# A two-layer block in split single precision: the rows of both operand buffers start at other addresses

## What is computed

```python
h = rms_norm(r, g_mix); z = h @ w_in                     # q, k, v, conv and gate columns
attn = moba_attention(q, k, v)                           # 8 heads of 128, one block of 256 keys
r = r + (sigmoid(g_a) * (attn @ w_attn_out) + sigmoid(g_c) * (conv @ w_conv_out)) @ w_o
r = r + square(relu(rms_norm(r, g_mlp) @ w_up)) @ w_down # width 8192
r = r + sigmoid(rms_norm(r, g_ple) @ w_ple_gate) * (p @ w_ple_proj)
# second layer, 16 more tokens ahead of the 256
u = conformer_conv(h)        # h @ conv_w_in, gate, 31 taps in time, layer norm, silu, @ conv_w_out
r = r + swiglu(h)            # (silu(h @ ffn_w_gate) * (h @ ffn_w_up)) @ ffn_w_down, width 5632
```

## Time and profile before

| | |
|---|---|
| three runs | 2543.49, 2543.50, 2542.21 us, median 2543.49 |
| profiled execution | span 2542.0 us from first to last instruction; 1.49 us less than the median of the runs. No other time is given for this execution |
| busy | PE 2523.6 us (99%), weight loads 2224.7 (88%), DVE 1722.5 (68%), ACT 1252.9 (49%), POOL 431.3 (17%) |
| read from HBM | 463 MB, 183 GB/s over the span |

### The profile page before, as it was taken

One profiled execution on the slowest core, in us unless ns is written; L12 is line 12 of the kernel. 1 busy time (PEld: TensorE's weight loads), 2 busy tenths in 40 slices (PEclk: granted clock), 3 DMA queues, 4 the chain that ended last, 5 costly groups with the idle time before them and its releaser, 6 DMA issues.

```text
span 2542.0 us, 42618 instructions
## 1 busy us (share of the span) xinstructions
PE 2523.6 (99%) x14605; PEld 2224.7 (88%) x14605; DVE 1722.5 (68%) x2097; ACT 1252.9 (49%) x1554; POOL 431.3 (17%) x291
## 2 busy tenths in 40 slices
PE   9999999999999999999999999999999999999998
PEld 8888888888888888888888899988888888888887
DVE  6568875587665665665667889985766556654665
ACT  6456555554544444444444554555644444444443
POOL 0034410002100000000002368973400000000001
PEclk9999999999999999999999999999999999999999
DMA  7655565665556666656565566536466656556554
GB/s 235 185 168 180 165 189 181 197 194 178 188 183 192 187 188 189 189 190 189 183 193 185 183 171 170 166 109 206 150 197 200 195 177 198 185 191 187 183 182 163
DMA packets 470962, 466.38 MB, mean 183 GB/s; under 512 B 14522, under 2 KB 441012, under 8 KB 470708
## 3 DMA queue, kind: packets, MB, share of 16 engines
q1 hardware_dynamic: 470336, 464.97, 59.1%
q10 hardware_dynamic: 546, 0.38, 0.1%
HBM read 463.20 MB, written 2.10 MB: 183 GB/s over the span
## 4 chain that ended last, share of the span: by engine, by line
PE 90%; DVE 8%; issue 1%; ACT 1%; POOL 0%; DMA 0%; DVEq 0%; POOLq 0%; ACTq 0%
PE gp L450 49%; PE gp L453 22%; DVE xp L1839 6%; PE gp L818 3%; PE gp L816 3%; PE gp L817 3%; PE gp L459 3%; PE gp L488 1%; PE gp L630 1%; PE gp L631 1%; PE gp L490 1%; PE gp L632 1%; PE xp L777 0%; DVE gp L1804 0%; DVE wlo L1423 0%
## 5 line engine op out<-in xcount | busy, mean ns | idle before, releaser
L1423 DVE TENSOR_TENSOR wlo<-stage,whi 128x1024 fp32r<-128x1024 f32 x809 | 1010.0, 1263 | 676.3 <-ACT whi L879 670.7
L879 ACT ACTIVATE whi<-stage 128x1024 fp32r<-128x1024 f32 x874 | 914.1, 1057 | 929.0 <-PE gp L453 601.7
L450 PE MATMUL gp<-A,whi 128*128 128x512 f32 x3968 | 1320.5, 393 | 0.3 <-DVE A L1530 0.3
L453 PE MATMUL gp<-A,wlo 128*128 128x256 f32 x3264 | 915.1, 280 | 0.0
L450 PEld LDWEIGHTS gp<-A,whi 128*128 128x128 f32 x3968 | 739.1, 188 | 164.1 <-DVE A L1530 0.7
L453 PEld LDWEIGHTS gp<-A,wlo 128*128 128x128 f32 x3264 | 614.5, 188 | 0.0
L450 PE MATMUL gp<-B,whi 128*128 128x512 f32 x1536 | 536.3, 394 | 0.6 <-issue 0.6
L453 PE MATMUL gp<-B,wlo 128*128 128x256 f32 x1536 | 430.5, 280 | 0.0
L450 PEld LDWEIGHTS gp<-B,whi 128*128 128x128 f32 x1536 | 287.7, 187 | 66.8 <-issue 1.0
L453 PEld LDWEIGHTS gp<-B,wlo 128*128 128x128 f32 x1536 | 290.2, 189 | 0.0
L2144 POOL TENSOR_TENSOR sq<-r 128x512 f32 x24 | 29.5, 1228 | 795.7 <-DVE r L1733 757.9
(11 more groups left out here) (324 smaller groups left out, 2143.5 us busy)
## 6 DMA issues: line engine op xcount, KB each, us to landing
stage<-in_w_in SPq DMA_DIRECT2D x160, 512.0 KB, 4.1
stage<-in_w_up SPq DMA_DIRECT2D x128, 512.0 KB, 3.8
stage<-in_w_down SPq DMA_DIRECT2D x128, 512.0 KB, 3.6
stage<-in_ffn_w_gate SPq DMA_DIRECT2D x88, 512.0 KB, 4.5
stage<-in_ffn_w_up SPq DMA_DIRECT2D x88, 512.0 KB, 4.4
stage<-in_ffn_w_down SPq DMA_DIRECT2D x88, 512.0 KB, 4.5
stage<-in_conv_w_in SPq DMA_DIRECT2D x64, 512.0 KB, 4.1
stage<-in_w_o SPq DMA_DIRECT2D x32, 512.0 KB, 4.4
```

The source lines that it names most:

```text
L450: nc.tensor.matmul(bank.rearrange("p (a t) -> p a t", a=2), hi, both_parts(M, kt), start=first, stop=False)
L453: done = nc.tensor.matmul(bank[:, T:2 * T], lo, M[:, kt, 0:T], start=False, stop=last)
L879: nc.scalar.activation(unit_homes(n, slot)[0], stage[:, slot, :], ACT.Copy).then_inc(hi_ready, 1)
L1423: nc.vector.tensor_tensor(lo, stage[:, slot, :], hi.bitcast(F32), ALU.subtract).then_inc(lo_ready, 1)
```

## The change

Each row of `A` becomes 548 words (2192 bytes in place of 2176) and each row of `B` 520 words (2080 in place of 2048). The low half stays at the same distance behind the high half. `both_parts` and `sq_parts` cut off the added words, so every instruction reads and writes as many elements as before, in the same order on each engine. Counted from the start of its buffer, row kt of `A` moves back by 16·kt bytes, row kt of `B` by 32·kt bytes. All that lies behind `A` moves by 256 bytes, and all behind `B` by 768 bytes in sum.

```diff
-        A = sb("A", [P, KT, 2 * TM], F32R)
-        B = sb("B", [P, KT, 2 * T], F32R)
+        A = sb("A", [P, KT, 2 * TM + 4], F32R)
+        B = sb("B", [P, KT, 2 * T + 8], F32R)
...
-        sq_parts = B[:, KT - 2:KT, :]
+        sq_parts = B[:, KT - 2:KT, 0:2 * T]
...
         def both_parts(M, kt):

-            return M[:, kt, :].rearrange("p (a t) -> p a t", a=2)[:, :, 0:T]
+            return M[:, kt, 0:2 * (TM if M is A else T)].rearrange("p (a t) -> p a t", a=2)[:, :, 0:T]
```

## The result

The changed kernel takes 2556.38 us (median of 4 runs, 2553.85 to 2556.78) against 2543.49 us before (4 runs, 2542.21 to 2543.67): a ratio of 1.005, 95% interval 1.0038 to 1.0062. It is slower by 12.9 us; the forecast was +1.9 us, the range held it. The profiled execution took 2556.09 us with a span of 2554.3 us, 12.3 us more than the span before.

What follows compares the result with a forecast made beforehand. The prediction took PE as the bound, the time being the sum of distances between matmuls. Its parts, −0.7 for B's pairs and +2.6 for back, the rest 0, gave +1.9 us on 2543.5: 2545.4 us, range 2518 to 2580.

Steps and rivals of the forecast that it cites:

- spread costs what A and v show: Whole kernel: spread rows of B take the distances that A's pairs and v's weights show; +1.9 us, chance 0.35.
- line of 5.1 us: Whole kernel: about 0.2%, what a measurement can tell from no change; slower than that was given 0.33.
- Pairs with B: 1536 pairs reading B: all take A's 348.4 ns, together −0.7 us, bounds −3.3 and +7.3.
- Pairs with A: 4096 pairs reading A: spread already, so 0, bounds −9.4 and +18.9 us.
- back: 1008 matmuls with rows of B stationary: 2.6 ns longer each, +2.6 us, bounds 0 and +2.6.
- v: 192 matmuls with rows of A stationary: 0, bounds −0.5 us and 0.
- conv2: Conv2's tiles, where the chain runs on DVE's taps: 0; with 3.4 ns on each matmul, +2 us.
- Other engines: DVE ops writing A and transfers into `stage`: hidden under PE, 0.
- Faster: All phases: differing starts break the slow rhythms and settle at the best distance seen; −13.2 us, 2530 us, chance 0.31.
- Slower: All pairs run like up's slow first round, 353.6 ns; +31 us, 2574 us, chance 0.28.
- harsher form: Pairs with A and B: starts between multiples of 64 bytes cost an extra piece, 6.7 ns; 2616 us.
- Addresses do nothing: Whole kernel: row places don't matter and differences are rhythm alone; 2543.5 us, chance 0.06.

Runs made afterwards that it cites:

- the moved starts alone: Kernel before with 64 unused words behind A and 128 behind B, rows unchanged: 2543.46 us, ratio 1.000.
- `B` alone moved: Kernel before with only B's rows eight words longer, A's rows unchanged: 2549.25 us, ratio 1.0025.
- `A` alone: Kernel before with only A's rows four words longer, B's rows unchanged: 2548.48 us, ratio 1.0017.
- the rows at multiples of 64 bytes: Kernel before with rows of A and B 16 words longer and a DMA scratch of 1024 bytes: 2555.23 us, ratio 1.0047.
- `A` at one place: Kernel before with A's rows of 2304 bytes, low half right behind the high half, B unchanged: 2543.34 us, ratio 1.0002.

## Why the prediction was right in kind and short in size

The reading of the bound held: no wait, transfer or other engine came into play but for PE's pause in conv2, and the time is the sum of distances that depend on where rows lie. The forecast "spread costs what A and v show" is the case that came, and the marks it set were met for up (349.5 to 349.9, "near 348 in all four rounds", a little high), down and glu (348 to 350), but not for back (232.7, "near 229"). The sum was +1.9 us in place of +12.3 in the profiles, and the time lies outside the forecast's own range (2540 to 2553) and inside the whole one. That the whole range held 2556.4 is luck as far as the forecast goes: its ends came from the rivals. By the prediction's own line of 5.1 us the kernel is slower, to which it gave 0.33, and 0.05 of that by the forecast's mechanism. By its steps:

1. *Pairs with B*: −0.7 forecast, +1.2 measured. Right that the quick pairs get slower and the slow ones quicker and nearly cancel. The size that was off is 348.4: it came out at 349.5. Both sums lean on the slow rhythm of up's first round in the profile before; against a quick one, as with the moved starts alone, that round would lose 0.75 us instead of gaining 0.95.
2. *Pairs with A*: 0 forecast, +3.4. The step that failed is "they are spread already". `A` had two places for its high halves, with its own mean, and got sixteen: down +1.4 ns a pair. Glu's later rounds lost nothing (−0.11 and −0.08 us), since their 350.2 was a rhythm of the two places (348.5 with `B` alone moved).
3. *back*: +2.6 forecast, +5.8. The largest miss, and it broke its bounds: the upper end was v's 229.4 ns, as if two places were the worst that a spread could do. Other places cost up to 234.3.
4. *v*: 0 forecast, with bounds at or below 0; +0.4. The same error.
5. *conv2*: 0 forecast; its distances are indeed hidden by DVE's taps (221.45 us with `A` alone). The +1.6 us came from the half clock behind a pause, which the prediction did not consider.
6. *Other engines*: 0, right.

So terms 2 to 4 failed for one reason: the two distances of rows with one and with two places were taken for the ends of a scale, "one place" and "spread". They are values at particular places. What the prediction lacked was the relation of the row to the weight tile; the rows of before could not show it, since there rows lay at place 0 or alternated between two places; moving the weight tiles shows it.

The rivals. *Faster*: where the profile before had the slow rhythm, the time fell (up's first round −0.95, gate −0.81 us), but the pairs settled between the good and the bad places, not at the best distance. *Slower*: its deciding point, a mean pair above 349.9 ns, was nearly reached (349.0 + 4.6 us / 5632 = 349.8), its 353.6 not; the loss over 5 us is back's and the clock's. Its harsher form fell with the rows at multiples of 64 bytes: up reads 350.0 ns there, no less than the 349.5 of rows off such multiples. *Addresses do nothing* fell with every kernel that moved a place; for shifts by multiples of 256 bytes it holds (ratio 1.000, 0.999 to 1.001).

Two rules that the prediction cited. The instructions of back are the same in both kernels, and only the place of the rows that are loaded as weights differs: 226.8 against 232.7 ns. The Trainium skill (TensorE: Matmul & The Clock Gate, Step-by-step) has the moving operand and the weight load on independent ports; here the distance depends on the places of both together, and the measurement decides. The Trainium skill (SBUF — State Buffer, Specifications) gives lines of 16 bytes. Rows touch as many of them before and after, since all start at multiples of 16 bytes, and the time is not the same. What in the chip makes a place good or bad no run here shows.

## What to carry to other kernels

When PE is the bound, read the distance from start to start, phase by phase: equal code with two distances is a rhythm, and a pad that looks harmless can move it. Padding rows by a few words spreads them over good and bad places; rows that are a multiple of 256 bytes apart keep one place against the weight tiles, and that place can be chosen by unused words ahead of the tiles (here 5.7 us, with as many matmuls of the same sizes in the same order). Bounds for a quantity with only two values in the trace should reach well past both, as two points say nothing of what lies outside them.

## What the runs showed of the hardware that was not expected

- The distance of packed-float32 matmuls at 2.4 GHz depends on the place of the row against the weight tile modulo 256 bytes: 226.8 to 234.3 ns for 512 columns with a new weight load each, 346.7 to 353.6 ns for a pair. Moving `B` by 256 and the weight tiles by 768 bytes changed nothing (ratio 1.000).
- At places 0 and 224 pairs run in one of two steady rhythms (346.7 or 353.6 ns), at place 64 too (348.9 or 353.3); a rhythm once set lasted for up to some 700 us (the quick one through all of up and down with `A` at one place) and across the change from one buffer to the other. What sets it at the start of a stretch wasn't tried.
- Behind a pause of PE of 2.2 to 2.8 us the granted clock stood at half for some 3.4 us in three profiles, and not in two others with a pause of 2.2 us. It cost 1.6 us.
